# Scatter and residual update of one expert moved into the next one's up phase, with w1 and w3 columns interleaved

## What is computed

```python
def swiglu(h, w1, w3, w2):
    return (jax.nn.silu(h @ w1) * (h @ w3)) @ w2

def moe_ffn(h, wr, br, w1, w3, w2):
    logits = (h @ wr).astype(jnp.float32) + br.astype(jnp.float32)
    top_v, top_i = lax.top_k(logits, TOP_K)
    top_w = jax.nn.softmax(top_v, axis=-1)
    gates = jnp.sum(jax.nn.one_hot(top_i, N_EXPERTS, dtype=jnp.float32) * top_w[..., None], axis=-2).astype(h.dtype)
    y = jnp.zeros_like(h)
    for e in range(N_EXPERTS):
        y = y + gates[..., e:e + 1] * swiglu(h, w1[e], w3[e], w2[e])
    return y
...
        x = x + mod_x[:, 5] * ffn(modulate(rms_norm(x, ffn_norm_g[i]), mod_x[:, 3], mod_x[:, 4]))
```

## Time and profile before

| | before |
|---|---|
| median of 3 runs | 1774.49 us |
| lowest and highest | 1768.44 and 1776.2 us |
| span of the profiled execution | 1772.8 us |
| busy in the span: TensorE matmuls, DVE, ACT, POOL | 93%, 25%, 17%, 2% |
| mean DMA rate over the span | 223 GB/s |
| instruction packets (queue 8) | 60, of 16 KB each |

### The profile page before, as it was taken

The page is one execution under the profiler, slowest core; times in us unless marked ns, Lnnn a source line. Parts: engine busy times, 40 slices in busy tenths (PEclk is TensorE's granted clock), DMA queues, the critical chain, the costliest instruction groups (busy, mean ns, idle before and its releaser), DMA issues.

```text
span 1772.8 us, 21037 instructions
## 1 busy us (share of the span) xinstructions
PE 1656.5 (93%) x7998; PEld 937.7 (53%) x7999; DVE 448.1 (25%) x1098; ACT 309.7 (17%) x721; POOL 43.0 (2%) x49
## 2 busy tenths in 40 slices
PE   3999879999999999999998999899989989999988
PEld 1454445444444444445665765685536555865464
DVE  1367794210000000003588330100201101001011
ACT  3135453210000000002345221000101010000110
POOL 1001000100000000000010100000000000000000
PEclk9999999999999999999999989999999999999999
DMA  9530610252141122115304269987799999977997
GB/s 379 223 143 0 246 41 25 89 223 91 71 166 71 71 73 93 71 71 231 125 11 180 73 255 422 390 291 278 292 420 421 422 422 422 377 269 290 422 421 324
DMA packets 56605, 394.76 MB, mean 223 GB/s; under 512 B 6480, under 2 KB 7888, under 8 KB 8912
## 3 DMA queue, kind: packets, MB, share of 16 engines
q1 hardware_dynamic: 56384, 393.63, 56.1%
q10 hardware_dynamic: 144, 0.01, 0.0%
HBM read 392.57 MB, written 1.05 MB: 222 GB/s over the span
## 4 chain that ended last, share of the span: by engine, by line
PE 79%; DMA 10%; DVE 7%; issue 2%; ACT 1%; SPq 1%; DVEq 0%; ACTq 0%
PE ps L688 17%; DMA ring<-in_stream 10%; PE ps L764 10%; PE ps L470 9%; PE ps L773 9%; PE ps L708 9%; PE ps L668 5%; PE ps L812 4%; PE ps L809 3%; PE ps L416 2%; PE ps L867 1%; PE ps L592 1%; PE ps L745 1%; PE ps L796 1%; DVE arena L1358 1%
## 5 line engine op out<-in xcount | busy, mean ns | idle before, releaser
L688 PE MATMUL ps<-hT,ring 128*128 128x512 f32 x704 | 302.7, 592 | 0.0
L764 PE MATMUL ps<-ring,arena 128*64 128x256 f32 x1056 | 243.2, 384 | 20.9 <-DMA ring<-in_stream 14.3
L767 PE MATMUL ps<-ring,arena 128*64 128x256 f32 x1056 | 243.7, 384 | 0.0
L688 PEld LDWEIGHTS ps<-hT,ring 128*128 128x128 f32 x704 | 133.5, 190 | 167.3 <-issue 166.4
L764 PEld LDWEIGHTS ps<-ring,arena 128*64 128x64 f32 x1056 | 139.9, 137 | 92.7 <-issue 33.6
L470 PE MATMUL ps<-hT,ring 128*128 128x512 f32 (+2 forms) x480 | 172.5, 515 | 2.4 <-ACT hT L921 2.2
L773 PE MATMUL ps<-ring,arena 128*128 128x256 f32 x704 | 155.6, 379 | 0.0
L708 PE MATMUL ps<-arena,ring 128*128 128x512 f32 x352 | 151.2, 592 | 0.0
L773 PEld LDWEIGHTS ps<-ring,arena 128*128 128x128 f32 x704 | 132.2, 190 | 17.1
L767 PEld LDWEIGHTS ps<-ring,arena 128*64 128x64 f32 x1056 | 140.0, 137 | 0.0
L470 PEld LDWEIGHTS ps<-hT,ring 128*128 128x128 f32 (+1 forms) x480 | 87.9, 185 | 81.7 <-issue 73.7
(11 more groups left out here) (188 smaller groups left out, 1345.7 us busy)
## 6 DMA issues: line engine op xcount, KB each, us to landing
ring<-in_stream SPq DMA_DIRECT2D x371, 1024.0 KB, 13.1
xT<-in_x SPq DMA_DIRECT2D x8, 256.0 KB, 4.2
cst<-in_consts SPq DMA_DIRECT2D x1, 1092.0 KB, 23.8
out_x<-xT SPq DMA_DIRECT2D x4, 256.0 KB, 2.6
par<-in_params SPq DMA_DIRECT2D x2, 75.0 KB, 2.3
cst<-in_consts SPq DMA_DIRECT2D x1, 128.5 KB, 2.2
moep<-in_moe SPq DMA_DIRECT2D x1, 36.0 KB, 25.5
ccol<-in_c ACTq DMA_DIRECT2D x1, 8.0 KB, 2.4
```

The source lines that it names most:

```text
L688: last = pe.matmul(ps[:, 2 * m + f % 2, :], ring[:, slot, m * 1024 + k * P:m * 1024 + (k + 1) * P], hT[:, k, :], start=(k == 0), stop=(k = ...
L764: a = pe.matmul(ps[0:64, b, 0:256], hTe[:, k, 0:64], ring[:, s1, k * 256:(k + 1) * 256], start=(k == 0), stop=(k == KD - 1))
L767: last = pe.matmul(ps[64:P, b, 0:256], hTe[:, k, 0:64], ring[:, s3, k * 256:(k + 1) * 256], start=(k == 0), stop=(k == KD - 1))
```

## The change

Weights: the units of the up phase hold, for four of the eight blocks of k each, 512 columns: 128 of w1, 128 of w3, 128 of w1, 128 of w3. A wide step is 8 matmuls of 128 x 512. A narrow step puts the first 256 of these columns on partitions 0 to 63 and the other 256 on 64 to 127. So silu and multiplication work on all 128 partitions and 128 columns, and one transposition turns the result. The first unit of a step is given back at its half.

Order: the copy of an item's output to `outE` stays behind its down phase. Its scatter and its residual update are done inside the up phase of the next item: four scatter matmuls after up step 1, four after up step 2, into banks 6 and 7; DVE does the updates between its multiplications. The turning of `selg` comes after up step 3, the last transposition after the gather. The first item scatters zeros, for which POOL clears `outE` and `selg_t`. The last item's scatter stands behind the loop. The scatter's code stands in both bodies and once more behind the loop.

```diff
+            def up(u, i, narrow):
+
+                b = u % 2
+                if u >= 2:
+                    pe.wait_ge(ge_done, i * U + (u - 1))
+                for half in range(2):
+                    s = unit_wait(2 * u + half, i)
+                    for kk in range(4):
+                        k = 4 * half + kk
+                        w = ring[:, s, kk * 512:(kk + 1) * 512]
+                        if narrow:
+
+                            for j in range(2):
+                                last = pe.matmul(ps[64 * j:64 * j + 64, b, 0:256], hTe[:, k, 0:64],
+                                                 w[:, j * 256:(j + 1) * 256], start=(k == 0), stop=(k == KD - 1))
+                                first(last)
+                        else:
+                            last = pe.matmul(ps[:, b, :], hTe[:, k, :], w, start=(k == 0), stop=(k == KD - 1))
+                            first(last)
+                    if half == 0:
+                        last.then_inc(ring_used, 1)
+                last.then_inc(eup_mm, 1)
+                owed[0] += 1
+
+            def turn_hidden(v, i, narrow):
+
+                pe.wait_ge(ge_done, i * U + (v + 1))
+                if v >= 2:
+                    pe.wait_ge(gte_done, i * U + (v - 1))
+                if narrow:
+                    last = pe.transpose(ps[:, 2 + v % 2, 0:P], g_e[:, v % 2, 0:P], c_("ident"))
+                else:
+                    for half in range(2):
+                        last = pe.transpose(ps[:, 2 + v % 2, half * P:(half + 1) * P],
+                                            g_e[:, v % 2, half * P:(half + 1) * P], c_("ident"))
+                last.then_inc(gt_mm, 1)
+
+            def scatter(bank0, d0, d1):
+
+                for d in range(d0, d1):
+                    last = pe.matmul(ps[:, bank0 + (d - d0) // 2, d % 2 * NX:(d % 2 + 1) * NX],
+                                     outE[:, d * P:(d + 1) * P], selg_t[:, :], start=True, stop=True)
+                    first(last)
+                    if d % 2:
+                        last.then_inc(scatter_mm, 1)
+
+            def turn_gates(i):
+
+                pe.wait_ge(y_done, i * 4 + 4)
+                for tt in range(2):
+                    last = pe.transpose(ps[:, 6, tt * P:(tt + 1) * P], selg[:, tt, :], c_("ident"))
+                last.then_inc(selgt_mm, 1)
+
...
+                    if u == U - 1 and n == 0:
+                        last.then_inc(acc_mm, 1)
+                last.then_inc(ring_used, 1)
...
             def expert(i, narrow):
-                for u in range(U + 1):
-                    if u < U:
-                        b = u % 2
-                        if u < 2:
-                            pe.wait_ge(y_done, i * 4 + (u + 1))
-                        else:
-                            pe.wait_ge(ge_done, i * U + (u - 1))
-                        if narrow:
...
+                up(0, i, narrow)
+                up(1, i, narrow)
+
+                pe.wait_ge(oute_act, i + 1)
+                pe.wait_ge(oute_dve, i + 1)
+                scatter(6, 0, 4)
+                turn_hidden(0, i, narrow)
+                up(2, i, narrow)
+                turn_hidden(1, i, narrow)
+                pe.wait_ge(y_done, i * 4 + 2)
+                scatter(6, 4, 8)
+                up(3, i, narrow)
+                turn_hidden(2, i, narrow)
+                turn_gates(i)
+                for u in range(4, U):
+                    up(u, i, narrow)
+                    turn_hidden(u - 1, i, narrow)
+                pe.wait_ge(selgt_done, i + 1)
                 pe.wait_ge(sel_ready, i + 2)
                 gather()
+                turn_hidden(U - 1, i, narrow)
                 for u in range(U):
+                    down(u, i, narrow)
...
-                pe.wait_ge(oute_act, i + 1)
-                pe.wait_ge(oute_dve, i + 1)
-                for d in range(KD):
-                    last = pe.matmul(ps[:, d // 2, d % 2 * NX:(d % 2 + 1) * NX], outE[:, d * P:(d + 1) * P], selg_t[:, :],
-                                     start=True, stop=True)
-                    if d == 0:
-                        first(last)
-                    if d % 2:
-                        last.then_inc(scatter_mm, 1)
+            pe.wait_ge(oute_act, n_items + 1)
+            pe.wait_ge(oute_dve, n_items + 1)
+            scatter(0, 0, KD)
...
+            def gate_up(u, i, narrow):
+
+                act.wait_ge(eup_mm, i * U + (u + 1))
+                if u >= 2:
+                    act.wait_ge(ge_done, i * U + (u - 1))
+                if narrow:
+                    act.activation(s_e[:, u % 2, 0:P], ps[:, u % 2, 0:P], ACT.Silu).then_inc(se_done, 1)
+                else:
+                    act.activation(s_e[:, u % 2, :].rearrange("p (a b) -> p a b", a=2),
+                                   ps[:, u % 2, :].rearrange("p (a b) -> p a b", a=2)[:, :, 0:P], ACT.Silu
+                                   ).then_inc(se_done, 1)
+
+            def keep_turned(v, i, narrow):
+
+                m = 64 if narrow else P
+                act.wait_ge(gt_mm, i * U + (v + 1))
+                act.activation(gTe[:, 2 * v:2 * v + 2, 0:m],
+                               ps[:, 2 + v % 2, 0:2 * m].rearrange("p (a b) -> p a b", a=2), ACT.Copy
+                               ).then_inc(gte_done, 1)
+
...
-            gps.memset(g_e, 0.0).then_inc(ge_zero, 1)
+            gps.memset(outE[:, 0:512], 0.0).then_inc(oute_act, 1)
+            gps.memset(outE[:, 512:1024], 0.0).then_inc(oute_dve, 1)
+            gps.memset(selg_t[:, :], 0.0).then_inc(first_clear, 1)
...
+            def add_scattered(i, b, bank):
+
+                dve.wait_ge(scatter_mm, i * 4 + (b + 1))
+                for k in (2 * b, 2 * b + 1):
+                    y = xT[:, k, 0:NX]
+                    last = dve.scalar_tensor_tensor(out=y, in0=ps[:, bank, k % 2 * NX:(k % 2 + 1) * NX],
+                                                    scalar=mod[:, 1, 0, 5 * KD + k:5 * KD + k + 1], in1=y,
+                                                    op0=ALU.mult, op1=ALU.add)
+                last.then_inc(y_done, 1)
+
+            def gated(u, i, narrow):
+
+                dve.wait_ge(se_done, i * U + (u + 1))
+                if u >= 2:
+                    dve.wait_ge(gt_mm, i * U + (u - 1))
+                if narrow:
+                    dve.tensor_tensor(g_e[:, u % 2, 0:P], ps[:, u % 2, P:2 * P], s_e[:, u % 2, 0:P], ALU.mult
+                                      ).then_inc(ge_done, 1)
+                else:
+                    dve.tensor_tensor(g_e[:, u % 2, :].rearrange("p (a b) -> p a b", a=2),
+                                      ps[:, u % 2, :].rearrange("p (a b) -> p a b", a=2)[:, :, P:2 * P],
+                                      s_e[:, u % 2, :].rearrange("p (a b) -> p a b", a=2), ALU.mult).then_inc(ge_done, 1)
+
...
+                gated(0, i, narrow)
+                gated(1, i, narrow)
+                for b in range(2):
+                    add_scattered(i, b, 6 + b % 2)
+                gated(2, i, narrow)
+                for b in range(2, 4):
+                    add_scattered(i, b, 6 + b % 2)
+                gated(3, i, narrow)
+                dve.wait_ge(selgt_mm, i + 1)
+                dve.tensor_copy(selg_t[:, :], ps[:, 6, 0:NX]).then_inc(selgt_done, 1)
+                pick(i + 1)
+                for u in range(4, U):
+                    gated(u, i, narrow)
...
-                dve.wait_ge(selgt_mm, i + 1)
-                dve.tensor_copy(selg_t[:, :], ps[:, 3, 0:NX]).then_inc(selgt_done, 1)
-                pick(i + 1)
...
-                dve.wait_ge(acc_mm, i + 1)
+                dve.wait_ge(ring_used, i * EXP_U + (FRONT + EXP_U))
                 dve.tensor_copy(outE[:, 512:1024], ps[:, 5, :]).then_inc(oute_dve, 1)
...
+            for b in range(4):
+                add_scattered(n_items, b, b)
...
-        ex[e, 0:22:2] = by_rows(x["moe_w1"][0, e], 256)
-        ex[e, 1:22:2] = by_rows(x["moe_w3"][0, e], 256)
+        up = np.stack([by_rows(x[w][0, e], P).reshape(UP_U, P, KD, P) for w in ("moe_w1", "moe_w3")])
+        up = up.reshape(2, UP_U // 2, 2, P, KD, P).transpose(1, 4, 3, 2, 0, 5)
+        ex[e, 0:22] = up.reshape(UP_U // 2, 2, 4, P, 512).transpose(0, 1, 3, 2, 4).reshape(UP_U, P, UNIT)
```

More of the change, by code:

```diff
@@ L1097, in _ @@
+            def expert(i, narrow):
+                gate_up(0, i, narrow)
+                for u in range(1, U):
+                    gate_up(u, i, narrow)
+                    keep_turned(u - 1, i, narrow)
+                keep_gathered(i)
+                keep_turned(U - 1, i, narrow)
             for b in range(4):
@@ L1498, in _ @@
                                                 in1=rtab("mask")[:, tt, :], op0=ALU.add, op1=ALU.mult)
[L1500 removed]
+            dve.tensor_copy(rtab("eight"), c_("eight"))
             dve.tensor_copy(rtab("count"), ps[:, 6, 2 * NE:3 * NE])
```

112 lines of the change are left out of this document (20 added, 92 removed).

## The result

The changed kernel takes 1745.7 us (median of 4 runs, 1744.4 to 1748.4) against 1775.4 us for the kernel before beside it: a ratio of 0.983, with a 95% interval of 0.981 to 0.985. The profiled execution has a span of 1746.5 us, against 1772.8 us before: the two profiles show 26.3 of the 29.6 us between the medians.

A forecast was written before the change was run, and what follows sets the result against it. Items 0, 1 and 5 were taken as TensorE-bound, items 2 to 4 and 6 to 7 as DMA-bound. Gains 4.2 + 10.9 + 0.7 + 8.2 - 1 = 23 us off the 1774.5 us median gave 1751 us, range 1742 to 1769.

The forecast's parts named there:

- the runs A and B: Narrow items behind a wide one, 2 to 4 and 6 to 7: DMA-bound, 12.9 and 10.2 us lost at their starts.
- The transpositions, the wide steps, the scatter: Transpositions save 1.2 us a narrow item; wide up steps change 0; scatter still takes 3.5 us, now also in item 0.
- The border 0 to 1: Border behind item 0: 12.7 us becomes 4.0, one fetch of 3.1 plus about 0.9 of half clock.
- The runs: Starts of items 2 to 4 and 6 to 7: DMA loses about 2 us each, gaining 10.9 and 8.2 us.
- Does the loop's code stay in the store?: TensorE's loop: 1676 recorded instructions after the change, 2018 before, fit its store, so no instruction packets after item 1.
- Steps 2, 4 and 6: Border 0 to 1 falls to 4.0 us; items 2 to 4 gain 10.9 us; items 6 and 7 gain 8.2 us.
- My border sum, 0.9 + 3.7 + 2.6: Border from wide to narrow, 7.2 us: 0.9 copy, 3.7 scatter, 2.6 gap in front of the first narrow matmul.
- The first rival: Each jump between bodies still fetches code: sum of gains only 10.7 us, 1764 us; chance 0.27.
- the end: Last scatter, code behind the loop: a missing block costs up to 4.5 us less 0.9; 1 us loss taken.

The follow-up runs named there:

- the late return: Kernel before with the interleaved columns alone, but both units of a narrow step given back at its end: 1762.0 us, ratio 0.993.
- the first two experiments: Kernel before with interleaved columns, scatter still at the border: 1754.6 us, 0.989; changed kernel with old columns, scatter moved: 1759.4 us, 0.992.

## Why the prediction was right, point by point

**What bounds the kernel.** Right. Items 0, 1 and 5 follow TensorE, the runs A and B follow DMA and its standstill at their start. The tripled scatter shows it: it costs its full 7 us in items 0 and 5 and less than half of its work in the runs.

**The transpositions, the wide steps, the scatter.** Item 0 took 68.6 us against a forecast of 69.2. Item 5 gained 1.6 instead of 0.7: it began 0.56 us late for its first unit instead of 0.8, and the rest of the difference was not looked into.

**The border 0 to 1.** 3.51 us of gap against 3.1, and 1.7 us of half clock (item 1 took 124.9 us, item 5 123.2 behind its wait) against 0.9.

**The runs.** DMA lost 2.1 and 1.8 us at their starts, 2 were forecast; run A took 229.0 against 229.9, run B 146.3 against 146.5. TensorE's waits for the ring are still there, 14.0 us in the up phases alone (row above), so the runs stayed bound by DMA.

**"Does the loop's code stay in the store?" This step failed.** It forecast no instruction packets after item 1, and they came at each change of body, which the prediction itself names as a sign of being wrong. The count of 1676 recorded instructions against 2018 did not tell it. Nor did the other argument, that before the change nearly all of the code stayed because the border behind item 6 was short: the trace of the kernel before has four packets in item 5, two in the border to item 6 and four in item 6 (DMA view of 1490.5 to 1665). The bodies were fetched anew, and only the border behind item 6 was free of it:

```profile
...
q8 instruction: 10, 0.16, 0.4%
```

Steps 2, 4 and 6 of the sum rest on this step. That steps 4 and 6 came out right all the same is luck in the mechanism: the fetches did not go away, they were hidden. The prediction had no term for how far TensorE's sequencer runs ahead of its matmuls. Without a wait ahead of the jump it asks for the other body's code while the down matmuls are still queued, and behind the wide items all of the fetch falls under these and the first matmuls of the next item. With the wait and nothing behind it, the queue is empty when the jump comes: 8.1 us of gap, two fetches in it. The wait ahead of the jump takes back nearly all of the change; the same wait behind the jump takes about 1 us. Behind item 0 the fetch is not hidden, though nothing waits ahead of the jump there either, and 3.5 us stay: its first packet starts 0.9 us before the last down matmul ends, behind item 1 5.9 us before. A likely reason, worked out from rows 7 and 8 and not tried: down matmuls last 0.22 us a record in a narrow item and 0.43 in a wide one, so that as many queued ones cover half the time.

In the kernel before, the border behind item 1 was 7.2 us with eight scatter matmuls in it; with the wait alone and no scatter it is 8.1. So its length was that of the copy, the jump and the fetches, and the scatter lay inside them. My border sum, 0.9 + 3.7 + 2.6, took the scatter for a term of its own, and it gave the right length of the gap by construction.

The Trainium skill ("Runtime: NRT & Kernel Launch", Instruction fetch mechanics) says that a taken branch out of the window forces a fetch before execution can go on. The runs with a wait ahead of the jump agree (two packets in a gap of 8.1 us); what the changed kernel adds is that the matmuls already queued go on meanwhile (two packets between 1230 and 1238.9 and no gap). The first rival, which had the fetches go on and gave 1764 us, was right about the packets and wrong about their price.

**The size.** 23 us forecast, 26 between the profiles, 29.6 between the medians. 1 us of the difference is the end, whose fetch did not show; 1 each is in item 5 and run A. The profiled execution of the changed kernel is the slowest of its four timed ones, 2.7 us over their median, which is most of why the medians lie further apart than the profiles.

**How much each part carries.** The prediction did not split its sum between the two parts; before the first two experiments I expected nearly all of it from the move. Measured: the interleaving alone gives 20 us and the move alone 15. Why the interleaving removes idle time at borders that still have their wait is shown in part. Its early return is worth 5 to 8 us, through the ring and, behind item 0, through the sequencer's earlier arrival at the jump. The rest goes with shorter gaps around the scatter, which are there with the late return too: 4.23 us instead of 3.09 and 4.54 behind item 0, and behind item 1 1.31 instead of 2.71, with a granted clock of 1.00 after it instead of 0.77. Why the fetches fall more kindly was argued, not tried: the wide body is 352 recorded instructions shorter, but the borders of the 16 KB blocks also lie elsewhere in the code, and neither was varied by itself. The same holds for the return of the last down unit at once, which came with the move and was never tried alone. The two kernels with the longer wide body also spread more from run to run (the one before 1768 to 1784 us in 49 runs, the move alone 1753 to 1777 in 12, against 1744 to 1750 for the changed one in 14); that too is seen and not explained.

## What to carry to other kernels

In a loop with branches, look for what the engine waits for right before it jumps, and for what is still queued when it jumps. A wait with nothing queued behind it is paid twice, once for itself and once for the code that is fetched after it: 8.1 us here. The same wait behind the jump costs 0.97 us, and with 3.7 us of matmuls between wait and jump 1.4 us of gap were left. A unit of weights that lands late holds up the jump in the same way.

Where a stream through a ring bounds a stretch, count how long DMA stands still at its start, not how long the engines take inside it: the first slots that come back set the time of everything behind them. And when two edits are made together, run each alone: here they gained 20 and 15 us alone and 29 together.

## What the hardware showed that I had not expected

- A jump back into the same body costs TensorE some 1.5 us when its queue is empty, even when no code is fetched: 2.45 us of gap, less 0.97 for the copy that it waited for. The jump to the other body, with two packets of 16 KB in the gap, takes 8.1 us, less the same 0.97.
- A gap of 8.1 us is followed by matmuls at the lower clock: in the 4.73 us behind it the granted clock is 0.58. A gap of 3.5 us behind item 0 of the changed kernel cost 1.7 us in the same way (row below); the gap of 1.42 us of the interleaved columns alone did not, with 1.00 behind it.

```profile
...
1114.08:1118.00 3.92, 3.92 (x5) 1.64 (x6) 0.00 (x0) 0.00 (x0) 0.00 (x0) 0.56 1.00 414
```
- The move alone has a code stall between two narrow items (4.88 us) in run B and none in run A. Which code stays in the store from one item to the next doesn't follow from the counts that I used.
